# Float32 conditioning matmuls in four column groups, spread singly; small matmuls in twos; w_out in two parts

## The chip, the cores and the metric

The kernel runs on one core of one Trainium2 chip. The metric is the device time of one execution in microseconds. Nothing else runs on the chip.

## The reference: what is computed

One inference step of a one-layer decoder, for a prompt of 256 tokens and 8 sample sequences of 4 tokens, 288 tokens in all, D = 2048, everything in float32. Two recurrent mixers (HGRN2 with 16 heads, mLSTM with 8) run side by side on the input projection:

```
mod = silu(c) @ ada_w + ada_b              # c: 9 rows (prompt, 8 samples); ada_w 2048 x 12288
sh1, sc1, g1, sh2, sc2, g2 = split(mod, 6)
h = rms_norm(x) * (1 + sc1) + sh1
proj = h @ w_in                            # 2048 x 18448, split into q, f, i, g, mq, mk, mv, ...
y_a = head_norm(hgrn2(...)) * silu(hg)     # per head: state 128 x 128
y_b = head_norm(mlstm(...)) * sigmoid(mo)  # per head: state 128 x 256
merged = sigmoid(ga) * y_a + sigmoid(gb) * y_b
x = x + g1 * (merged @ w_out)              # w_out 2048 x 2048
h = rms_norm(x) * (1 + sc2) + sh2
a, g = split(h @ w_up, 2)                  # 2048 x 11264
x = x + g2 * ((gelu(conv3(a) + cb) * g) @ w_down)      # 5632 x 2048
y = rms_norm(x, final_norm_w)              # and the states after the step are outputs too
```

## The kernel before

Tokens stand along the free axis: T = 288 columns. Every weight is read once from DRAM, in chunks of 512 KB: 4 contraction tiles of 128 rows (KC) by 256 weight columns (CN), a float32 tile of 128 x 1024. SyncE issues the chunks in a fixed order into a ring `raw` of 4 slots. One block is 4 chunks: the whole contraction of 2048 for 256 output columns.

A block of kind "s" is a projection of the tokens. Its products are split in three: ScalarE makes `whi`, a copy rounded to the matmul type float32r (L781), VectorE the rest `wlo = raw - whi` (L1111), three chunks ahead of TensorE (LEAD), and TensorE does three passes per 128 x 128 weight tile, hi by hi, lo by hi, hi by lo, 24 passes of 288 columns a chunk (L449, L450, L451). A block of kind "a" is conditioning: 256 columns of ada_w, also split by both engines, in 8 passes of 256 columns a chunk (L463, with 18 stationary columns `cs`, the hi and lo parts of silu(c)). The sums land in `ps`, ScalarE copies them to `arows` (L784), `ada_turn` (L473) adds hi and lo and turns rows into columns by a product with `sel`, and VectorE adds the bias into `mod`. Slot `k % 4` of `raw` is loaded again when VectorE has made the `wlo` of the chunk four before it, for both kinds.

There are 584 s chunks and 192 a chunks. The stages, in order:

- ada1: 64 a chunks (sh1 and sc1), with the transposes of x in the first half;
- hg0 to hg3: one group of four HGRN heads each, 40 s and 8 a chunks; the heads of a group are worked off in the next stage;
- ml0 to ml3: two mLSTM heads each, 32 s and 16 a chunks; ml0 works off the last four HGRN heads, ml1 to ml3 two mLSTM heads each;
- ada2: 32 a chunks, with the last two mLSTM heads;
- out: w_out, 32 s chunks; up: 22 loops of 8 s chunks; down: 88 s chunks; then the final norm and the output.

A head is cut into steps (10 for HGRN, 12 for mLSTM), which TensorE, ScalarE, VectorE and GpSimd take at the same chunk numbers (`steps_at` spaces them evenly). TensorE's steps are generators, which yield after each small matmul: `chunk` takes one between two weight tiles, 7 a chunk, and `drain` issues all that is left at the chunk's end. Small matmuls are plain float32. The PSUM tensor `R` has 4 banks for them. The order is written out by hand on every engine; semaphores join the engines.

```
if s == 1 and b and kinds[b - 1] == "a":
    ada_turn(A0 + ada_before(b - 1, kinds), (b - 1) % 2)
drain(due)
if hook is not None:
    due = hook(k)
```

Names that come back below: `cs` stationary columns of the conditioning, `landed` DMA arrived, `lo_done` VectorE's `wlo` made, `used` TensorE done with a chunk, `bank_free` a `ps` bank read out, `Vx`/`Vxs` masked copies of a head's values for the state update, `Sst` the states of a head's 8 sub-chunks.

## Time and profile before

| | |
|---|---|
| three runs | 2757.1, 2760.88, 2763.0 us; median 2760.88 us |
| the profiled execution: its own time | 2762.37 us |
| its span | 2760.8 us |
| mean granted TensorE clock | 0.932 of full |
| TensorE busy | 2586.7 us, 94% |
| VectorE, ScalarE, GpSimd busy | 1397.2, 1285.5, 458.1 us |

TensorE is the engine that the others feed. The window rows below give for each stage its length, the busy time of TensorE, the granted clock and the share of DMA; a pass is one weight tile moved against 288 (or 256) columns, and a plain float32 matmul shows as two passes. The columns of a window row are: from and to, length, busy time (and instructions) of TensorE's matmuls, its weight loads, VectorE, ScalarE and GpSimd, granted clock, DMA share, GB/s. A timeline row has the start, the duration, engine, line, operation and tiles, output rows, the moved tile, and in brackets the idle time before it and what ended that. In a timeline row, the start of a pass less the start of the one before it is what that one costs on the path.

### The profile page before, as it was taken

To read this page: it belongs to the slowest core of one execution; us is meant where nothing else is said; L and a number is where in the kernel's file an instruction comes from. 1 tells how busy PE (TensorE), PEld (TensorE's weight loads), DVE (VectorE), ACT (ScalarE), POOL (GpSimd) and SP (SyncE) were. 2 spreads that over 40 slices of the span, in tenths; PEclk is the share of its full clock that TensorE was granted. 3 is DMA by queue.
4 is the path that set the end of the run, shared out by engine and by line. 5 is a ranking of instruction groups with operands and counts; after the bars stand their busy time and mean duration, and the time that the engine had idled before them with its cause. 6 is when DMAs were issued, how large, how long until landed. Compare 5 with 4: busy or idle time off the path is not lost.

```text
span 2760.8 us, 46789 instructions
## 1 busy us (share of the span) xinstructions
PE 2586.7 (94%) x17745; PEld 2383.9 (86%) x17745; DVE 1397.2 (51%) x1602; ACT 1285.5 (47%) x1577; POOL 458.1 (17%) x514
## 2 busy tenths in 40 slices
PE   5779999999999999999999989898999999999997
PEld 3559988888888988888888876798999999999997
DVE  4554454354344455555565456555555555544443
...
GB/s 228 269 127 203 175 161 132 140 154 138 132 154 140 146 167 164 177 178 170 153 185 192 171 170 204 178 161 158 166 167 160 167 159 172 163 199 162 168 168 89
DMA packets 424717, 460.08 MB, mean 167 GB/s; under 512 B 16676, under 2 KB 414412, under 8 KB 423330
## 3 DMA queue, kind: packets, MB, share of 16 engines
...
q14 instruction: 30, 0.25, 0.0%
...
## 4 chain that ended last, share of the span: by engine, by line
PE 79%; issue 7%; DVE 4%; DMA 4%; ACT 3%; POOL 2%; ACTq 1%; POOLq 0%; DVEq 0%; SPq 0%
PE ps L449 22%; PE ps L450 21%; PE ps L451 21%; DMA raw<-in_ada_w 2%; PE ps L463 2%; DVE wlo L1111 2%; PE R L429 1%; ACT whi L781 1%; PE R L592 1%; PE R L576 1%; PE R L653 1%; PE R L598 1%; PE R L600 1%; PE R L586 1%; PE ps L473 1%
## 5 line engine op out<-in xcount | busy, mean ns | idle before, releaser
L1111 DVE TENSOR_TENSOR wlo<-raw,whi 128x1024 fp32r<-128x1024 f32 x776 | 1036.0, 1352 | 863.4 <-ACT whi L781 848.4
L449 PE MATMUL ps<-xh,whi 128*128 128x288 f32 x3968 | 1238.7, 312 | 47.7 <-issue 29.7
L450 PE MATMUL ps<-xl,whi 128*128 128x288 f32 x3968 | 1192.4, 301 | 0.0
L451 PE MATMUL ps<-xh,wlo 128*128 128x288 f32 x3968 | 1192.1, 300 | 0.0
L781 ACT ACTIVATE whi<-raw 128x1024 fp32r<-128x1024 f32 x776 | 808.5, 1055 | 781.4 <-PE ps L451 649.2
L449 PEld LDWEIGHTS ps<-xh,whi 128*128 128x128 f32 x3968 | 769.6, 194 | 81.5 <-issue 58.7
L450 PEld LDWEIGHTS ps<-xl,whi 128*128 128x128 f32 x3968 | 767.3, 193 | 16.7 <-issue 15.1
L451 PEld LDWEIGHTS ps<-xh,wlo 128*128 128x128 f32 x3968 | 767.2, 193 | 0.0
L463 PE MATMUL ps<-whi,cs 128*18 128x256 f32 x768 | 216.6, 313 | 10.2 <-DVE wlo L1111 10.1
L463 PE MATMUL ps<-wlo,cs 128*18 128x256 f32 x768 | 212.4, 308 | 0.0
L450 PE MATMUL ps<-ffl,whi 128*128 128x288 f32 x704 | 208.4, 296 | 0.0
L451 PE MATMUL ps<-ffh,wlo 128*128 128x288 f32 x704 | 207.6, 295 | 0.0
L449 PE MATMUL ps<-ffh,whi 128*128 128x288 f32 x704 | 207.3, 295 | 0.0
L449 PEld LDWEIGHTS ps<-ffh,whi 128*128 128x128 f32 x704 | 132.5, 188 | 0.2
L450 PEld LDWEIGHTS ps<-ffl,whi 128*128 128x128 f32 x704 | 132.4, 188 | 0.0
L451 PEld LDWEIGHTS ps<-ffh,wlo 128*128 128x128 f32 x704 | 132.2, 188 | 0.0
L463 PEld LDWEIGHTS ps<-whi,cs 128*18 128x18 f32 x768 | 82.7, 108 | 54.5 <-issue 21.5
L463 PEld LDWEIGHTS ps<-wlo,cs 128*18 128x18 f32 x768 | 82.8, 108 | 22.1 <-issue 1.6
L1603 POOL COPY tails<-abuf 128x4 f32 x22 | 4.1, 187 | 421.0 <-ACT abuf L1068 421.0
L1252 DVE TENSOR_TENSOR S<-S,R 128x1024 f32<-128x1024 f32 x16 | 19.5, 1222 | 107.3 <-PE R L600 107.3
L903 ACT ACTIVATE S<-ps 128x576 f32<-128x576 f32 x40 | 26.0, 650 | 97.3 <-PE ps L451 97.3
L473 PEld LDWEIGHTS ps<-sel,arows 18*128 18x128 f32 x192 | 30.2, 222 | 40.1 <-ACT arows L784 32.1
...
## 6 DMA issues: line engine op xcount, KB each, us to landing
raw<-in_w_in SPq DMA_DIRECT2D x288, 512.0 KB, 4.0
raw<-in_ada_w SPq DMA_DIRECT2D x192, 512.0 KB, 4.7
raw<-in_w_up SPq DMA_DIRECT2D x176, 512.0 KB, 3.7
raw<-in_w_down SPq DMA_DIRECT2D x88, 512.0 KB, 3.7
raw<-in_w_out SPq DMA_DIRECT2D x32, 512.0 KB, 3.8
S<-in_state_hgrn POOLq DMA_DIRECT2D x16, 512.0 KB, 5.5
out<-S POOLq DMA_DIRECT2D x16, 512.0 KB, 4.3
...
```

The lines of the kernel that those rows point to most:

```text
L429: return nc.tensor.transpose(out, in_, ident[0:in_.shape[0], 0:in_.shape[0]])
L449: mm(o, whi[:, s, kk, cols], hi[:, kt0 + kk, :], start=first and kk == 0, stop=False)
L450: mm(o, whi[:, s, kk, cols], lo[:, kt0 + kk, :], start=False, stop=False)
L451: x = mm(o, wlo[:, s, kk, cols], hi[:, kt0 + kk, :], start=False, stop=last and kk == KC - 1)
L463: x = mm(ps[0:2 * NB, bank, 0, 0:CN], cs[:, kt0 + kk, :], w[:, s, kk, :], start=first and kk == 0 and w is whi, stop=last and kk == KC - 1 ...
L473: x = mm(ps[:, bank, 1, NB * m:NB * (m + 1)], arows[:, bank, P * m:P * (m + 1)], sel[:, :], start=True, stop=True)
L576: mm(R[:, bank, :], Kt[:, t, :], Vx[:, t].rearrange("p a b -> p (a b)"), start=True, stop=True).then_inc(hg["u"], 1)
L586: mm(R[:, 2, SUB * c:SUB * (c + 1)], Sst[:, c - 1, :], qs[:, SUB * c:SUB * (c + 1)], start=False, stop=False, skip_group_check=True)
L592: x = mm(R[:, 2, TP + LS * b:TP + LS * (b + 1)], S0[:, b, :], qt[:, TP + LS * b:TP + LS * (b + 1)], start=False, stop=b == NS - 1, skip_gr ...
L598: mm(R[:, 0, :], Kts[:, :], Vxs[:, 0:4, :].rearrange("p a b -> p (a b)"), start=True, stop=True)
L781: A(whi[:, s], raw[:, s], ACT.Copy).then_inc(hi_done, 1)
L1111: TT(wlo[:, s], raw[:, s], whi[:, s].bitcast(F32), ALU.subtract).then_inc(lo_done, 1)
```

## The change

- **Conditioning chunks.** An a chunk is no longer split. TensorE does 4 plain float32 matmuls of 256 columns (8 passes), with the contraction tile kk of the chunk into its own 32 output rows, `acc[32*kk:32*kk+32]`; `cs` is 32 wide, float32, 9 columns and zeros. It waits for the DMA alone (`landed`), and the slot of such a chunk is loaded again once TensorE has used it. ScalarE and VectorE do nothing for it. Outside ada1 the sums have a PSUM bank of their own, `ab`, so the mixers' `R` has 3 banks. `ada_turn` has contraction 128 instead of 18, and `sel` adds the four groups of rows.
- **Where they stand.** They come singly, after three s chunks or two, instead of in blocks of four: 12 in each HG stage (8 before), 12 in each ML stage (16 before), 32 in the first eight (double) loops of up (none before). Stage ada2 is gone. ada1 keeps its 64.
- **Small matmuls.** TensorE takes two small steps after every two weight tiles, 8 a chunk, and one after an a chunk. A step that isn't finished goes on in later chunks (`turns`); nothing is drained at a chunk's end. The chunk at which each step of a head is due on TensorE and on the other engines comes from tables: a head starts every 12 chunks in the HG stages, every 10 in ml0, 22 in ml1 to ml3, 11 in w_out.
- **w_out.** It comes in two parts: P1, 24 chunks, contraction tiles 0 to 11 for all eight column blocks, with the last two mLSTM heads worked off beside it; and P2, 8 chunks, tiles 12 to 15. VectorE scales P1's sums into `mixo`, and adds P2's in `second_part`, block by block; GpSimd adds `xT2`, the spilled x.
- Small: `dno` is 4 tiles instead of 16, some of the mixers' reads and order of banks differ, and an mLSTM head's first broadcast is cut in two.

The diff, cut to its core (the tables, SyncE's ring, TensorE's chunks and streams, and VectorE's w_out):

```diff
-HG_BLOCKS = "ssassssassss"
-ML_BLOCKS = "ssassassasas"
...
+HG_KINDS = "sssa" * 12 + "ssss"
+ML_KINDS = "sssa" + "sssassa" * 5 + "ssa" + "ss"
+UP_KINDS = "sssasssasssasssassss"
+THEN = "sss"
...
+HG_DUE = {0: 0, 1: 1, 2: 2, 3: 4, 5: 6, 6: 10, 7: 10, 8: 11, 9: 12}
+HG_DUE_PE = {2: 2, 4: 5, 6: 7, 8: 11}
+ML_DUE = {0: 0, 2: 3, 3: 5, 4: 6, 5: 8, 7: 14, 8: 16, 9: 18, 10: 19, 11: 20}
+ML_DUE_PE = {1: 1, 3: 4, 4: 6, 6: 9, 8: 16, 10: 19}
+OUT_DUE = {0: 0, 2: 2, 3: 3, 4: 4, 5: 5, 7: 9, 8: 10, 9: 11, 10: 11, 11: 12}
+OUT_DUE_PE = {1: 1, 3: 3, 4: 4, 6: 6, 8: 10, 10: 11}
+HG_TURNS = (2, 14, 26, 38)
+HG_TURNS_ML = (1, 11, 21, 31)
+ML_TURNS = (0, 22)
+OUT_TURNS = (0, 11)
...
-            def block256(N, b, view, col, chunks=4, first=False):
-
-                for s in range(chunks):
-                    k = chunks * b + s
+            def slot_free(N, k, kinds, tail):
+
+
+                if k >= RING:
+                    old, split = kinds[k - RING], before(kinds, k - RING + 1, "s")
+                else:
+                    old, split = tail[k], -tail[k + 1:].count("s")
+                if old == "s":
+                    sp.wait_ge(lo_done, N[2] + split)
+                else:
+                    sp.wait_ge(used, N[0] + k - RING + 1 + FREE)
...
+            def stage(N, kinds, tail, view, cols, a0=None, length=4, kt0=0):
+
+
+                for k, kind in enumerate(kinds):
+                    slot_free(N, k, kinds, tail)
+                    if kind == "s":
+                        q = before(kinds, k, "s")
+                        load(k, view, kt0 + KC * (q % length), cols[q // length])
+                    else:
+                        e = before(kinds, k, "a")
+                        load(k, ada_v, KC * (e % 4), CN * (a0 + e // 4))
...
-            def chunk(c, k, first, last, bank, hi, lo, kt0, steps=None):
-
-
-
-                pe.wait_ge(lo_done, c + 1)
+            def chunk(c, k, first, last, bank, hi, lo, kt0, steps, half=None):
+
+
+                pe.wait_ge(lo_done, c)
                 s = k % RING
                 for kk in range(KC):
+                    if half is not None and kk % 2 == 0:
+                        pe.wait_ge(xlo, half + kk // 2)
                     for m in range(2):
...
                         x = mm(o, wlo[:, s, kk, cols], hi[:, kt0 + kk, :], start=False, stop=last and kk == KC - 1)
                         if kk == KC - 1 and m == 1:
                             x.then_inc(used, 1)
-                        elif steps is not None:
-                            next(steps, None)
-
-            def ada_chunk(c, k, first, last, bank, kt0, steps):
-
-                pe.wait_ge(lo_done, c + 1)
+                    next(steps, None)
+                    next(steps, None)
+
+            def ada_chunk(c, k, first, last, acc, kt0):
+
+
                 s = k % RING
+                pe.wait_ge(landed[s], 4 * c + 16 * (k // RING + 1))
                 for kk in range(KC):
-                    for w in (whi, wlo):
-                        x = mm(ps[0:2 * NB, bank, 0, 0:CN], cs[:, kt0 + kk, :], w[:, s, kk, :], start=first and kk == 0 and w is whi,
-                               stop=last and kk == KC - 1 and w is wlo)
+                    x = mm(acc[32 * kk:32 * kk + 32, 0:CN], cs[:, kt0 + kk, :], raw[:, s, kk, :], start=first, stop=last)
                 x.then_inc(used, 1)
-                next(steps, None)
-                next(steps, None)
-
-            def ada_turn(n, bank):
+
+            def ada_turn(n, half, acc):
 
                 pe.wait_ge(ada_rows, n + 1)
                 for m in range(2):
-                    x = mm(ps[:, bank, 1, NB * m:NB * (m + 1)], arows[:, bank, P * m:P * (m + 1)], sel[:, :], start=True, stop=True)
+                    x = mm(acc[:, CN + NB * m:CN + NB * (m + 1)], arows[half][:, P * m:P * (m + 1)], sel[:, :], start=True, stop=True)
                 x.then_inc(ada_cols, 1)
...
-            def stream(N, kinds, A0, hook=None, xparts=None):
-
-
-                due = nothing()
-                for b, kind in enumerate(kinds):
-                    pe.wait_ge(bank_free[b % 2], N[1] + b // 2 + FREE)
-                    for s in range(4):
-                        k = 4 * b + s
+            now = [0]
+
+            def turns(order, step, head, i):
+
+
+                for k, j, o in order:
+                    while now[0] < k:
+                        yield
+                    yield from step(j, o, head + j, i)
+
+            def stream(N, kinds, a0=None, steps=None, length=4, kt0=0, xparts=None, halves=None):
+
+                steps = nothing() if steps is None else steps
+                for k, kind in enumerate(kinds):
+                    now[0] = k
+                    if kind == "s":
+                        q = before(kinds, k, "s")
+                        b, s = q // length, q % length
+                        if s == 0:
+                            pe.wait_ge(bank_free[b % 2], N[1] + b // 2 + FREE)
                         if xparts is not None and b == 0:
                             pe.wait_ge(xlo, xparts + s + 1)
-                        if kind == "s":
-                            chunk(N[0] + k, k, s == 0, s == 3, b % 2, xh, xl, KC * s, due)
-                        else:
-                            ada_chunk(N[0] + k, k, s == 0, s == 3, b % 2, KC * s, due)
-                        if s == 1 and b and kinds[b - 1] == "a":
-                            ada_turn(A0 + ada_before(b - 1, kinds), (b - 1) % 2)
-                        drain(due)
-                        if hook is not None:
-                            due = hook(k)
-                drain(due)
-                if kinds[-1] == "a":
-                    ada_turn(A0 + ada_before(len(kinds) - 1, kinds), (len(kinds) - 1) % 2)
+                        chunk(N[2] + q + 1, k, s == 0, s == length - 1, b % 2, xh, xl, kt0 + KC * s, steps, halves if q == 0 else None)
+                    else:
+                        e = before(kinds, k, "a")
+                        if e % 4 == 0:
+                            pe.wait_ge(ada_free, a0 - A_HG + e // 4 + FREE)
+                        ada_chunk(N[0], k, e % 4 == 0, e % 4 == 3, ab, KC * (e % 4))
+                        next(steps, None)
+                    if k >= 2 and kinds[k - 2] == "a" and before(kinds, k - 1, "a") % 4 == 0:
+                        ada_turn(a0 + before(kinds, k - 1, "a") // 4 - 1, 0, ab)
+                drain(steps)
+
...
+                stream(hg_base(i + 1), HG_KINDS, A_HG + 3 + 3 * i, turns(in_order(HG_TURNS, HG_DUE_PE), hg_step, 4 * i, i))
+            stream(ml_base(0), ML_KINDS, A_ML, turns(in_order(HG_TURNS_ML, HG_DUE_PE), hg_step, 12, 3))
...
-            def hook(k):
-                for j, o in ML_AT_ADA[k]:
-                    yield from ml_step(j, o, 6 + j, 3)
-            stream(ada2_base(0), "a" * 8, A_ADA2, hook)
-            pe.wait_ge(ml["c"], 4 * MH + FREE)
-            pe.wait_ge(ml["c2"], MH + FREE)
+                stream(ml_base(i + 1), ML_KINDS, A_ML + 3 + 3 * i, turns(in_order(ML_TURNS, ML_DUE_PE), ml_step, 2 * i, i))
+
+            stream(N_P1, "s" * 24, steps=turns(in_order(OUT_TURNS, OUT_DUE_PE), ml_step, 6, 3), length=3, xparts=4)
+            pe.wait_ge(ml["c2"], 4 * MH + FREE)
             nc.tensor.transpose(R[0:NB * MH, 1, 0:P], nnew[:].rearrange("p a b -> p (a b)"), ident[:, :]).then_inc(n_t, 1)
-
-            stream(out_base(0), "ss", 0, xparts=4)
-            with pe.Fori(1, 4) as i:
-                stream(out_base(i), "ss", 0)
+            stream(N_P2, "s" * 8, length=1, kt0=12, halves=8)
...
-            def stream(N, kinds, dst, hook):
-
-                for b, kind in enumerate(kinds):
-                    for s in range(4):
-                        k = 4 * b + s
+            def stream(N, kinds, dst=None, hook=None, each=None):
+
+                for k, kind in enumerate(kinds):
+                    if (kinds + THEN)[k + LEAD] == "s":
                         hi(N, k + LEAD)
...
+            def first_part(k, n):
+                if n % 3 == 2:
+                    u = n // 3
+                    if u == 0:
+                        dve.wait_ge(ml["sig"], 4 * 4)
+                        dve.wait_ge(ml["pre"], 2 * 4)
+                        dve.wait_ge(ada_free, 8 + FREE)
+                    b, kt = u % 2, slice(2 * u, 2 * u + 2)
+                    dve.wait_ge(used, N_P1[0] + k + 1 + FREE)
+                    TT(mixo[:, kt, 0:TP], ps[:, b, :, 0:TP], gate(u)[:, :, 0:1].to_broadcast([P, 2, TP]), ALU.mult).then_inc(x1_m, 1)
+                    TT(seq3(mixo[:, kt, TP:T], LS), seq3(ps[:, b, :, TP:T], LS), rep3(gate(u)[:, :, 1:NB], LS), ALU.mult).then_inc(bank_free[b], 1)
...
+            def second_part(k, u):
+                b, kt = u % 2, slice(2 * u, 2 * u + 2)
+                dve.wait_ge(used, N_P2[0] + k + 1 + FREE)
+                dve.wait_ge(x1_m, u + 1)
+                dve.wait_ge(bank_free[b], N_P1[1] + u // 2 + 1 + FREE)
+                for m in range(2):
+                    STT(mixo[:, 2 * u + m, 0:TP], ps[:, b, m, 0:TP], gate(u)[:, m, 0:1], mixo[:, 2 * u + m, 0:TP], ALU.mult, ALU.add).then_inc(x1_p, 1)
+                TT(seq3(x1s[:, b], LS), seq3(ps[:, b, :, TP:T], LS), rep3(gate(u)[:, :, 1:NB], LS), ALU.mult).then_inc(bank_free[b], 1)
+                dve.wait_ge(bank_free[b], N_P2[1] + u // 2 + 1 + FREE)
+                TT(mixo[:, kt, TP:T], mixo[:, kt, TP:T], x1s[:, b], ALU.add).then_inc(x1_p, 1)
+            stream(N_P2, "s" * 8, each=second_part)
```

Two places of TensorE's order. The first is in an HG stage, at the end of step 6 of a head and the first a chunk behind it. `R` holds the small results, `ps` and `ab` the streams' sums; in brackets are the semaphores waited for. Before:

```order
L583 MATMUL R<-PT,Vt 128x128
L586 MATMUL R<-qs,Sst 128x32 x7
L589 MATMUL R<-PTs,Vts 128x32
L592 MATMUL R<-qt,S 128x4 x8
L597 REGISTER_ALU
L598 MATMUL R<-Vxs,Kts 128x512 [waits hg_vx]
L600 MATMUL R<-Vxs,Kts 128x512
L459 REGISTER_ALU
L463 MATMUL ps<-whi,cs 18x256 [waits lo_done]
L463 MATMUL ps<-wlo,cs 18x256
```

The same place in the changed kernel (`xh`, `xl` are the split tokens):

```order
L654 MATMUL R<-qt,S 128x4 x2
L501 REGISTER_ALU
L503 MATMUL ab<-raw,cs 32x256 [waits landed3]
L503 MATMUL ab<-raw,cs 32x256 x3
L654 MATMUL R<-qt,S 128x4
L481 REGISTER_ALU
L489 MATMUL ps<-xh,whi 128x288 [waits lo_done]
L490 MATMUL ps<-xl,whi 128x288
L491 MATMUL ps<-xh,wlo 128x288
```

Before, the small matmuls ran out in one sequence and an a chunk followed, which waits for VectorE's `lo_done`; now two small ones precede the a chunk, which waits for the DMA, one follows it, and weight tiles of the projection come between the rest.

The second place is the first step of an mLSTM head whose work stood in ada2. Before:

```order
L463 MATMUL ps<-wlo,cs 18x256
L613 MATMUL R<-mLR,ones 128x512 [waits ml_c,ml_c2,ml_lr]
L615 MATMUL R<-mLR,ones 128x104
L617 MATMUL R<-mW 128x256 [waits ml_sig]
L619 MATMUL R<-mW 128x128
L621 MATMUL R<-mW 32x32
L429 MATMUL R<-ident,mW 128x128 x2
L429 MATMUL R<-ident,mW 32x128
L463 MATMUL ps<-whi,cs 18x256 [waits lo_done]
```

In the changed kernel it stands in P1 of w_out:

```order
L675 MATMUL R<-mLR,ones 128x328 [waits ml_c2,ml_lr]
L678 MATMUL R<-mW 128x256 [waits ml_sig]
L489 MATMUL ps<-xh,whi 128x288
L490 MATMUL ps<-xl,whi 128x288
L491 MATMUL ps<-xh,wlo 128x288
```

What moved: the head's first matmuls stood between passes of conditioning chunks, drained in one go; now two stand between weight tiles of w_out. An order row is one instruction: a plain float32 matmul is one row there and two passes in the trace.

## Rows read from the trace of the kernel before

**Rows 1.** The page: busy time, share of the span and instructions per engine.

```profile
PE 2586.7 (94%) x17745; PEld 2383.9 (86%) x17745; DVE 1397.2 (51%) x1602; ACT 1285.5 (47%) x1577; POOL 458.1 (17%) x514
```

**Rows 2.** The span in nine windows, one per stage (PEclk: mean granted clock).

```profile
28.80:189.00 160.20, 117.90 (x766) 86.19 (x767) 100.20 (x105) 99.61 (x130) 19.40 (x18) 0.82 0.74 235
189.00:332.80 143.80, 139.53 (x1040) 136.38 (x1038) 63.46 (x66) 62.14 (x75) 2.00 (x5) 0.99 0.61 174
332.80:953.90 621.10, 589.87 (x3793) 529.28 (x3794) 281.13 (x354) 289.98 (x377) 171.77 (x175) 0.90 0.48 142
953.90:1135.90 182.00, 174.78 (x1146) 152.99 (x1145) 93.97 (x121) 95.79 (x126) 57.09 (x58) 0.92 0.55 164
1135.90:1645.90 510.00, 494.05 (x3296) 443.57 (x3295) 279.44 (x271) 225.69 (x294) 103.93 (x54) 0.95 0.57 176
1645.90:1761.80 115.90, 97.77 (x477) 69.12 (x476) 70.76 (x80) 58.84 (x83) 31.88 (x20) 0.72 0.60 190
1761.80:1887.00 125.20, 110.69 (x785) 108.97 (x785) 66.97 (x71) 48.77 (x52) 10.20 (x6) 0.94 0.53 178
1887.00:2449.80 562.80, 562.80 (x4224) 562.80 (x4225) 306.39 (x398) 290.65 (x318) 31.43 (x111) 1.00 0.53 163
2449.80:2760.80 311.00, 296.62 (x2210) 292.18 (x2208) 132.84 (x135) 107.22 (x115) 23.55 (x32) 0.97 0.49 156
```

**Rows 3.** TensorE in order of time: passes of conditioning chunks, stage ada1.

```profile
34.61 0.28 PE L463 MATMUL ps<-whi,cs 128*18 128x256 f32 x1
...
35.43 0.28 PE L463 MATMUL ps<-wlo,cs 128*18 128x256 f32 x1
```

**Rows 4.** TensorE in order of time: a float32 matmul of 288 columns.

```profile
384.75 0.65 PE L603 MATMUL R<-lf,ones 128*128 128x288 f32 x2
...
385.37 0.29 PE L450 MATMUL ps<-xl,whi 128*128 128x288 f32 x1
```

**Rows 5.** TensorE in order of time: a float32 matmul with 32 output rows.

```profile
400.36 0.29 PE L451 MATMUL ps<-xh,wlo 128*128 128x288 f32 x1
400.58 0.25 PE L562 MATMUL R<-qt,kt_ 128*32 128x32 f32 x2
```

**Rows 6.** TensorE in order of time: a float32 matmul of contraction 32.

```profile
1200.05 1.12 PE L674 MATMUL R<-mVx,mK 32*128 32x512 f32 x2
...
1201.34 0.29 PE L450 MATMUL ps<-xl,whi 128*128 128x288 f32 x1
```

**Rows 7.** TensorE in order of time: small matmuls before the clock fell.

```profile
367.69 0.71 PE L583 MATMUL R<-PT,Vt 128*128 128x128 f32 x4 [1.91 <-DVE Sst L1248]
...
371.04 3.58 PE L592 MATMUL R<-qt,S 128*128 128x4 f32 x16
...
378.45 0.42 PE L463 MATMUL ps<-wlo,cs 128*18 128x256 f32 x1
```

**Rows 8.** The clock in two windows around that place.

```profile
366.00:378.20 12.20, 10.52 (x40) 7.88 (x40) 3.68 (x7) 1.35 (x2) 1.91 (x1) 0.62 0.42 129
382.90:398.00 15.10, 15.10 (x113) 14.81 (x112) 5.92 (x8) 9.74 (x13) 2.25 (x3) 1.00 0.65 202
```

**Rows 9.** TensorE in order of time: idle times, loop end and ada2.

```profile
540.89 0.40 PE L449 MATMUL ps<-xh,whi 128*128 128x288 f32 x1 [6.67 <-issue]
...
1658.58 2.07 PE L613 MATMUL R<-mLR,ones 8*128 8x512 f32 x2 [6.25 <-DVE mLR L1261]
```

**Rows 10.** Groups by line: split passes, and two producers of a head.

```profile
L1111 DVE TENSOR_TENSOR wlo<-raw,whi 128x1024 fp32r<-128x1024 f32 x776 | 1036.0, 1352 | 863.4 <-ACT whi L781 848.4 <-DMA xT<-xT_spill 9.5 <-DMA out<-Sst 2.6
L781 ACT ACTIVATE whi<-raw 128x1024 fp32r<-128x1024 f32 x776 | 808.5, 1055 | 781.4 <-PE ps L451 649.2 <-DMA raw<-in_w_in 51.1 <-DMA raw<-in_ada_w 42.1
...
L1504 POOL COPY Vx<-Vt 32x256 f32<-32x256 f32 x64 | 45.3, 707 | 48.1 <-ACT Kts L944 45.3
...
L1248 DVE SCALAR_TENSOR_TENSOR Sst<-Sst,dec,R 128x128 f32<-128x128 f32 x112 | 39.0, 348 | 4.0
```

**Rows 11.** DMA issues: KB each and us to landing, ada_w chunks.

```profile
raw<-in_ada_w SPq DMA_DIRECT2D x192, 512.0 KB, 4.7
```

More of the change, by code:

```diff
@@ L103, in down_base @@
 def down_base(i):
-    return ahead(N_DOWN, i, 44, 2)
+    return ahead(N_DOWN, i, 44, 2, 44)
 A_HG = 16
-A_ML = A_HG + 4 * HG_BLOCKS.count("a")
-A_ADA2 = A_ML + 4 * ML_BLOCKS.count("a")
-def ada_before(b, kinds):
-    return kinds[:b].count("a")
-HG_NSTEP = 10
-ML_NSTEP = 12
-def steps_at(k, first, chunks, nsteps, heads):
-    return [(j, o) for j in range(heads) for o in range(nsteps)
-            if first + (j * nsteps + o) * (chunks - first) // (heads * nsteps) == k]
+A_ML = A_HG + 4 * 3
+A_UP = A_ML + 4 * 3
@@ new lines, in down_stage @@
+            def down_stage(i):
+                stage(down_base(i), "s" * 44, "ssss", down_v, [1024 * i + CN * u for u in range(4)], length=11)
+            ada1_stage(0, first=True)
+            with sp.Fori(1, 8) as i:
+                ada1_stage(i)
+            hg_stage(0, "aaaa")
+            with sp.Fori(1, 4) as i:
+                hg_stage(i, HG_KINDS[-4:])
+            ml_stage(0, HG_KINDS[-4:])
+            with sp.Fori(1, 4) as i:
+                ml_stage(i, ML_KINDS[-4:])
+            stage(N_P1, "s" * 24, ML_KINDS[-4:], out_v, [CN * u for u in range(8)], length=3)
@@ L405, in _ @@
+            stage(N_P2, "s" * 8, "ssss", out_v, [CN * u for u in range(8)], length=1, kt0=12)
+            with sp.Fori(0, 8) as i:
+                stage(up2_base(i), UP_KINDS, "ssss", up_v, [FF * u + CN * (2 * i + p) for p in range(2) for u in range(2)], A_UP + i)
+            with sp.Fori(0, 6) as i:
+                stage(up1_base(i), "s" * 8, "ssss", up_v, [FF * u + CN * (16 + i) for u in range(2)])
             with sp.Fori(0, 2) as i:
-                for u in range(4):
-                    block256(down_base(i), u, down_v, 1024 * i + CN * u, chunks=11)
+                down_stage(i)
@@ L858, in ada1 @@
                     A(merged[:, bass.ds(4 * i, 4), :], xT[:, bass.ds(4 * i, 4), :], ACT.Square).then_inc(sq_done, 1)
-            for k in range(LEAD):
-                hi(N_ADA1, k, first=True)
-            ada1(0, True, first=True)
-            with act.Fori(1, 4) as i:
+            with act.Fori(0, 4) as i:
                 ada1(i, True)
@@ L876, in _ @@
                 ada1(i, False)
+            for k in range(LEAD):
+                hi(N_HG, k)
             modulate(1, merged, 0, KT)
@@ L1059, in _, with up_stream, each @@
             act.wait_ge(spill_1, 16)
-            with act.Fori(0, 22) as i:
-                for k in range(8):
-                    hi(up_base(i), k + LEAD)
-                    if k == 3:
-                        act.wait_ge(used, up_base(i)[0] + 4 + FREE)
+            def up_stream(N, kinds, first):
+                def each(k, n):
+                    i = first + n // 8
+                    if n % 8 == 3:
+                        act.wait_ge(used, N[0] + k + 1 + FREE)
                         act.wait_ge(ff_conv, 6 * i + FREE)
@@ L1354, in _, with up_stream, each @@
             cw = [par[:, 2, 0:44], par[:, 2, 44:88], par[:, 3, 0:44]]
-            with dve.Fori(0, 22) as i:
-                for k in range(8):
-                    lo(up_base(i), k + LEAD)
-                    if k == 4:
+            def up_stream(N, kinds, a0, first):
+                def each(k, n):
+                    i = first + n // 8
+                    if n % 8 == 4:
                         dve.wait_ge(bank_free[0], N_UP[1] + i + 1 + FREE)
```

647 lines of the change are left out of this document (331 added, 316 removed).

## The prediction

> **What bounds the kernel now.** I read the page first: TensorE is busy 94% of the span, VectorE 51%, ScalarE 47% [rows 1]. Then the nine windows by stage [rows 2]. The reader is to see three things in them. In up, TensorE runs without an idle moment at the full clock, and 562.8 us for 4224 passes is 0.133 us a pass: a chunk of 24 passes costs 3.20 us, and nothing but fewer passes helps. In ada1 it is busy 118 of 160 us: the weights' transfers and their splits set the pace. Between lie the stages with heads, where the clock stands at 0.90 to 0.95, in ada2 at 0.72, and some idle time remains. Two sums tell what is lost there. Length times (1 - clock) is at most 62 us in hg1 to hg3, 15 in ml0, 25 in ml1 to ml3, 32 in ada2. Length less busy time is 31, 7, 16 and 18 us. Where the clock falls is seen in the timeline: after a head's small matmuls, 16 passes of 4 columns in 3.58 us among them, the next conditioning pass is at half speed (0.42 us for 0.28), in a window with a granted clock of 0.62, the level of 1.2 GHz for most of it; beside projection passes it is 1.00 (2.4 GHz) [rows 3, 7, 8]. So what counts is TensorE's time: its passes, its clock, and what it waits for.
>
> **An a chunk.** Before, 8 passes. From one pass to another seven later are 0.82 us, 0.117 each, so 0.93 us a chunk [rows 3]. In the change there are 8 passes too, but of plain float32. Their price: from the start of a 288-column float32 matmul to the second projection pass behind it are 0.62 us; less one pass of 0.133, that is 0.484 for two passes, 0.24 each, two clock cycles a column [rows 4]. For 256 columns that is 0.2135 us, and 8 in sequence would be 1.71. No row shows matmuls with different groups of output rows behind each other. Upper bound: all in sequence, and going over to 32 output rows and back at the dearest switch in the trace. That is the one to contraction 32: 1.29 us from its start to the second pass behind it, less 0.133, and 0.09 before it as below, against 2 x 0.427 by columns, so 0.39 [rows 6]; sum 2.10. Lower bound: the four groups all beside each other, two passes and 0.11: 0.54. The switch I take at 0.11 in and out, since the trace has one to 32 output rows: the matmul starts 0.22 after the pass before it instead of 0.133, so 0.09 for the way in [rows 5]; the way back had hardly a cost there. For overlap I take the middle, an assumption of mine: a matmul's second pass goes to the same rows as its first and waits for it, but the next matmul's first pass is free to run beside it. That is 5 slots for 8 passes, 5 x 0.2135 + 0.11 = **1.18 us**.
>
> The Trainium skill, "TensorEngine Tiling (Array Packing)", Key Properties, says that a change of tiling mode drains the array; that speaks against 128 a chunks put singly between 128-wide passes, and the trace agrees that a switch costs, 0.09 and 0.39 us [rows 5, 6]. By the dearer one for each, the sum would be 36 us worse. Every 0.1 us of an a chunk is 12.8 us for the 128 outside ada1.
>
> **Stage by stage.**
> - ada1: the splits go. Before, a slot was free again after 4.7 us of transfer [rows 11], 1.06 of `whi` and 1.35 of `wlo` [rows 10]: 7.1 us for four slots, 1.78 a chunk. 235 GB/s at a share of 0.74 are 318 at most, 1.65 us a chunk [rows 2]. 64 x 0.13 = 8 is the least gain, the stage's whole DMA idle time, 0.26 x 160 = 42, the most; x's transposes, the norm and the gates stay. I take -15.
> - hg0: 8 a chunks at 0.93 become 12 at 1.18: +7. Its clock is 0.99 [rows 2], nothing to gain.
> - hg1 to hg3: 24 become 36: 42.5 - 22.3 = +20. Twos in place of ones, and no drain at a chunk's end, make switches more: three for each stage of them at 0.39, +4. Back comes the clock: small matmuls stand between six projection passes, not in bursts; of 62 us I take 45, since the tiny passes remain. The waits: of 31 idle us, 6.7 at each of three loop ends stay (the engine issues nothing there) [rows 9]; a head's wait for `Sst` (1.91) [rows 7] goes behind projection chunks; -9. Sum -30.
> - ml0: 16 become 12, -1; four turns at contraction 18 lose the switch of 0.39, -2; clock -11 of 15; waits -3 of 7: -17.
> - ml1 to ml3: 48 become 36, 42.5 - 44.6 = -2; twelve turns -5; clock -18 of 25; waits -5 of 16 (a chunks no longer wait for `wlo`): -30.
> - ada2 and out: 32 x 0.93 = 30 moved out, its eight turns too (-6), its idle time of 18, which begins with 6.25 us on `mLR` [rows 9], and 25 of 32 us of clock; the two heads' passes now lie in P1. Added: 3 us to split the merged tiles before P1, 5 at P1 to P2 (the last head's output to the last split, TensorE has nothing else), 1 for VectorE's three operations a block in P2 where a chunk's 3.2 us must cover them, 2 for switches. -79 + 11 = -68.
> - up: 32 x 1.18 + 8 turns at 0.43 (two float32 matmuls) = +41. Nothing hides it: TensorE has no gap there [rows 2].
> - down: nothing; its `dno` has a wait more, two blocks (70 us) behind.
>
> Sum: -15 + 7 - 30 - 17 - 30 - 68 + 41 = -112. The profiled execution took 2762.4 us, its span 2760.8, the median is 2760.9; so 2650 by either.
>
> **New waits.** An a chunk's slot comes free with TensorE, not three chunks ahead of it. An s chunk loaded there lands 4.7 us later and is needed split (2.4 more) about 7.6 us after it, two projection chunks and an a chunk on: it is just in time, in ML stages too. Queued behind a late one on ScalarE and VectorE are the heads' steps. A head's step 4 on TensorE stands 5 chunks from its start and waits for four `Vx` at 0.71 us; step 6, seven from it, for eight of `Sst` at 0.35 [rows 10]; between stand 16 and 6.4 us of projection, more than these.
>
> **Rivals.**
> - The a passes run in sequence, switches cheap: 1.82 a chunk, 128 x 0.64 = +82, and ada1's gain halved, +8: 2740. For it: no row shows two float32 passes beside each other. Against: they use different output rows.
> - Slower: in sequence with the dear switch, 2.10 a chunk, 128 x 0.92 = +118 and all of ada1's gain: **2780**. The place is TensorE in each single a chunk; it decides from about 2.05 a chunk. For it: 0.39 is what the trace has for a switch that also narrows the array [rows 6]. Against: 0.09 for 32 output rows [rows 5].
> - Full overlap: 0.56 a chunk, -79: 2570. The four matmuls would start together. The Trainium skill, "TensorE: Matmul & The Clock Gate", Part 3, has packed matmuls start some 4 ns apart; no run here shows it.
> - The tables don't fit: steps come before their operands, and TensorE, with everything in order behind it, waits at each. From 4.6 us a head over 24 heads the gain is gone; at 5, 2770. For it: PSUM has a bank less, and a row of steps on other engines stands before each wait. Against: the 16 us above.
> - The clock stays low: half of the 99 us of it don't come, and a few waits: 2705. For it: there are as many tiny passes as before.
>
> **How the numbers follow.** Chances: forecast 0.50 (its own range 2600 to 2705, from 0.8 to 1.6 a chunk), in sequence 0.15, slower 0.12, full overlap 0.06, tables 0.09, clock 0.08. The predicted time is the likeliest's, 2650. The range, 2580 to 2775, leaves out full overlap and the slower case, 18 in 100. About 0.2%, 5.5 us, is what a measurement of this kernel can tell. Faster holds the forecast, sequence, full overlap and clock cases but for 0.02 of the second: 0.77; slower the 0.12 and half of the tables' 0.09: 0.17; the rest 0.06.
>
> **What would show it.** In the changed profile: from the pass before an a chunk to the pass behind it, 1.2 us right, 1.8 or 2.1 for the rivals; up's window 604 us long, at clock 1.00; PEclk of hg1 to hg3 at 0.97 or more; no idle time before `whi` or L489 beyond 1 us outside the loop ends; ada1 at 145; ada2 and out together 173. What makes it wrong: an a chunk off by 0.5 us, or waits of 5 us and more per head behind Sst, Vx or the state updates.

## The result, and the profile after

The changed kernel takes 2779.1 us (median of 20 runs, 2759.5 to 2805.7), the kernel before 2762.0 beside it (2743.4 to 2780.2): a ratio of 1.0053, 95% interval 1.0028 to 1.0078. It is half a per cent slower; I had forecast 2650.

The page of the changed kernel, busy time per engine, which answers to [rows 1]:

```profile
PE 2519.8 (91%) x17745; PEld 2257.8 (81%) x17745; DVE 1144.0 (41%) x1435; ACT 1055.7 (38%) x1351; POOL 426.1 (15%) x524
```

TensorE is busy 67 us less than before, ScalarE 230 and VectorE 253 us less, and the span is 22 us longer: 2782.9. The engines have less to do and TensorE waits more. The windows of its stages, ada1, hg0, hg1 to hg3, ml0, ml1 to ml3, w_out (P1 and P2), up, down, with the columns of [rows 2]:

```profile
24.90:166.20 141.30, 100.84 (x768) 45.49 (x768) 22.01 (x45) 39.68 (x72) 13.97 (x18) 0.66 0.82 266
166.20:311.50 145.30, 140.20 (x1077) 132.89 (x1075) 54.30 (x59) 54.74 (x68) 2.04 (x5) 0.99 0.61 186
311.50:932.70 621.20, 572.51 (x3900) 506.69 (x3901) 254.26 (x333) 268.88 (x356) 141.04 (x175) 0.95 0.49 153
932.70:1127.80 195.10, 167.40 (x1110) 143.46 (x1108) 68.18 (x102) 73.13 (x104) 52.81 (x57) 0.92 0.45 142
1127.80:1677.60 549.80, 486.07 (x3188) 417.79 (x3188) 206.24 (x223) 182.79 (x247) 95.94 (x56) 0.92 0.48 152
1677.60:1880.90 203.30, 162.89 (x971) 144.98 (x971) 98.47 (x134) 69.68 (x92) 57.32 (x34) 0.87 0.40 131
1880.90:2471.60 590.70, 590.66 (x4513) 572.06 (x4514) 307.29 (x406) 255.89 (x298) 32.15 (x111) 1.00 0.58 184
2471.60:2782.90 311.30, 296.60 (x2210) 291.97 (x2208) 132.82 (x135) 107.45 (x115) 23.57 (x32) 0.98 0.49 156
```

Against [rows 2] and against the forecast, in us (the last column is the kernel of the third experiment, below):

| stage | before | forecast | after | both edits |
|---|---|---|---|---|
| ada1 | 160.2 | -15 | -18.9 | -17.3 |
| hg0 | 143.8 | +7 | +1.5 | -0.5 |
| hg1 to hg3 | 621.1 | -30 | +0.1 | -35.6 |
| ml0 | 182.0 | -17 | +13.1 | +3.7 |
| ml1 to ml3 | 510.0 | -30 | +39.8 | -40.3 |
| ada2 and out | 241.1 | -68 | -37.8 | -60.8 |
| up | 562.8 | +41 | +27.9 | +28.4 |
| down | 311.0 | 0 | +0.3 | +1.0 |
| before ada1 | 28.8 | 0 | -3.9 | -2.8 |
| sum | | -112 | +22.1 | -124.2 |

So the forecast comes near where there are no heads (ada1, hg0, up, down: at most 13 us off) and fails where there are. In hg1 to hg3 TensorE is busy 17 us less than before and idle 49 us instead of 31, which cancels; in ml1 to ml3 it is busy 8 us less and idle 64 us instead of 16.

What a single conditioning chunk costs, in up, TensorE in order of time:

```profile
1891.90 0.29 PE L491 MATMUL ps<-xh,wlo 128*128 128x288 f32 x1
1892.12 0.64 PE L503 MATMUL ab<-raw,cs 128*32 128x256 f32 x8
1892.69 0.40 PE L489 MATMUL ps<-xh,whi 128*128 128x288 f32 x1
1892.93 0.30 PE L490 MATMUL ps<-xl,whi 128*128 128x288 f32 x1
```

From the projection pass before it (1891.90) to the second behind it (1892.93) are 1.03 us; two passes of 0.133 belong to the projection, so the chunk costs 0.76: 0.09 to go over, 0.57 for the 8 passes, 0.11 to come back. 32 x 0.76 and 8 turns at the forecast's 0.43 are 28 us, what up has grown by.

What TensorE waited for (us in total, times, longest), the rows that matter here:

```profile
PE R L625 <- DVE kt_ L1301: 33.1, 14, 3.3
PE R L729 <- ACT hsq L1054: 27.7, 8, 4.4
...
PE R L675 <- DVE mLR L1328: 18.5, 4, 6.4
PE R L640 <- POOL Vx L1601: 16.5, 13, 6.3
...
PE R L742 <- ACT dn L1059: 10.8, 5, 4.0
```

In the same view of the kernel before, the first four of these operands stand at 3.4, 7.0, 6.3 and 9.0 us, and `dn` not at all (`kt_` belongs to an HGRN head's step 2, `mLR` to an mLSTM head's first step, `hsq` and `dn` to its late ones). And ScalarE, waiting for the weights of the projection before it can make `whi`: 237 us, where [rows 10] had 51.

```profile
ACT whi L839 <- DMA raw<-in_w_in: 237.1, 74, 9.4
```

**One wait followed back.** The longest wait for `mLR` is at the second head of an ML stage. TensorE, SyncE's queue, ScalarE and VectorE in order of time:

```profile
1217.05 0.64 PE L503 MATMUL ab<-raw,cs 128*32 128x256 f32 x8
...
1221.57 0.29 PE L491 MATMUL ps<-xh,wlo 128*128 128x288 f32 x1
1228.23 1.45 PE L675 MATMUL R<-mLR,ones 8*128 8x328 f32 x2 [6.37 <-DVE mLR L1328]
```

```profile
1217.89 2.19 SPq L401 DMA_DIRECT2D raw<-in_w_in  x3
```

```profile
1225.35 1.06 ACT L839 ACTIVATE whi<-raw 128x1024 fp32r<-128x1024 f32 x1 [7.54 <-DMA raw<-in_w_in]
```

```profile
1226.44 1.22 DVE L1175 TENSOR_TENSOR wlo<-raw,whi 128x1024 fp32r<-128x1024 f32 x1 [9.79 <-ACT whi L839]
1227.58 0.52 DVE L1328 TENSOR_SCALAR mLR<-LR,ident 8x616 f32<-8x616 f32 x1
```

The reader is to see the order. TensorE ends a conditioning chunk at 1217.7. Only then is its slot of the ring free, and SyncE, whose queue stood at that slot, issues three loads at once (1217.89), two of them into slots whose chunks had been split before. They share the DMA with a head's stores (GpSimd issues one of 1 MB at 1217.30); from 1217.9 to 1225.4 the DMA share is 0.91, at 300 GB/s, and the first load is there 7.5 us after its issue. What the stores and what the other two loads have in that, no run separates. ScalarE splits it at 1225.35, VectorE at 1226.44, and only behind that, in VectorE's written order, comes the small `mLR` that TensorE has been waiting for since 1221.9. It starts at 1228.23.

**What a wait does to the clock.** The same place in windows, the wait and the stretch behind it, and one 12 us later:

```profile
1222.00:1228.20 6.20, 0.00 (x0) 0.00 (x0) 1.76 (x3) 2.11 (x2) 0.90 (x1) 0.78 1.04 330
1228.20:1240.00 11.80, 11.77 (x61) 9.76 (x62) 2.88 (x5) 2.01 (x5) 0.00 (x0) 0.68 0.30 102
1240.00:1250.00 10.00, 10.00 (x77) 8.88 (x76) 3.30 (x6) 4.24 (x8) 0.00 (x0) 1.00 0.54 169
```

Behind the wait of 6.4 us the granted clock is 0.68 for 12 us, at 1.2 GHz for more than half of it, then 1.00 again: 11.8 x 0.32 = 3.8 us are lost on top of the wait itself.

**A wait that has nothing to do with transfers.** In the HG stages TensorE waits 2.75 us for `kt_` in nine of twelve heads. ScalarE and TensorE at one of them:

```profile
366.38 1.05 ACT L839 ACTIVATE whi<-raw 128x1024 fp32r<-128x1024 f32 x1
367.44 1.28 ACT L990 ACT_TABLE_LOAD   x1
368.73 0.63 ACT L990 ACTIVATE lf<-W,onec,lbc 128x288 f32<-128x288 f32 x1
369.27 0.63 ACT L960 ACTIVATE S<-ps 128x576 f32<-128x576 f32 x1
369.80 1.05 ACT L839 ACTIVATE whi<-raw 128x1024 fp32r<-128x1024 f32 x1
370.86 1.28 ACT L994 ACT_TABLE_LOAD   x1
372.16 0.44 ACT L994 ACTIVATE e<-bm 128x288 f32<-128x288 f32 x1
```

```profile
374.09 0.48 PE L625 MATMUL R<-qt,kt_ 128*128 128x128 f32 x2 [2.75 <-DVE kt_ L1301]
```

ScalarE has no idle time here: two table loads of 1.28 us, three copies for the streams, the logarithm and the exponentials, one behind the other; `qt` and `kt_` on VectorE follow. TensorE's step 2 is due two chunks after the head's start, and the chunk between is a conditioning chunk of 0.76 us.

### The profile page after: what moved, and what is told of

It is laid out like the page before. It is cut to its first block and busy times, and to the rows that moved or that the text cites. A ratio compares the mean times of both kernels' runs of the same rounds, so it can differ in the third digit from the quotient of the medians.

```text
span 2782.9 us, 45708 instructions
## 1 busy us (share of the span) xinstructions
PE 2519.8 (91%) x17745; PEld 2257.8 (81%) x17745; DVE 1144.0 (41%) x1435; ACT 1055.7 (38%) x1351; POOL 426.1 (15%) x524
## 5 line engine op out<-in xcount | busy, mean ns | idle before, releaser
L489 PE MATMUL ps<-xh,whi 128*128 128x288 f32 x3968 | 1273.1, 321 | 37.2 <-issue 24.5
L1175 DVE TENSOR_TENSOR wlo<-raw,whi 128x1024 fp32r<-128x1024 f32 x584 | 769.6, 1321 | 1210.0 <-ACT whi L839 1208.6
L839 ACT ACTIVATE whi<-raw 128x1024 fp32r<-128x1024 f32 x584 | 615.2, 1056 | 1153.6 <-PE ps L491 783.0
L503 PE MATMUL ab<-raw,cs 128*32 128x256 f32 x1024 | 83.1, 397 | 3.8 <-DVE mod L1190 3.8
L503 PE MATMUL ps<-raw,cs 128*32 128x256 f32 x512 | 58.7, 571 | 23.1 <-DMA raw<-in_ada_w 22.7
L1605 POOL TENSOR_TENSOR S<-S,e 128x1024 f32<-128x1024 f32 x16 | 34.1, 2128 | 268.4 <-PE R L654 268.4
L1632 POOL TENSOR_TENSOR mVx<-mV,bmask 32x2048 f32<-32x2048 f32 x8 | 31.1, 3891 | 167.5 <-ACT mV L1048 167.5
L503 PEld LDWEIGHTS ps<-raw,cs 128*32 128x32 f32 x512 | 14.4, 137 | 51.8 <-DMA raw<-in_ada_w 43.9
L640 PE MATMUL R<-Vx,Kt 128*128 128x512 f32 x64 | 37.3, 679 | 16.5 <-POOL Vx L1601 16.5
```

The source lines that it names most:

```text
L489: mm(o, whi[:, s, kk, cols], hi[:, kt0 + kk, :], start=first and kk == 0, stop=False)
L503: x = mm(acc[32 * kk:32 * kk + 32, 0:CN], cs[:, kt0 + kk, :], raw[:, s, kk, :], start=first, stop=last)
L640: mm(R[:, t, :], Kt[:, t, :], Vx[:, t].rearrange("p a b -> p (a b)"), start=True, stop=True).then_inc(hg["u"], 1)
L839: A(whi[:, s], raw[:, s], ACT.Copy).then_inc(hi_done, 1)
L1175: TT(wlo[:, s], raw[:, s], whi[:, s].bitcast(F32), ALU.subtract).then_inc(lo_done, 1)
L1605: G(S0[:, :, :], S0[:, :, :], seq(e1[:, TP:T], LS)[:, :, LS - 1:LS].to_broadcast([P, NS, P]), ALU.mult).then_inc(hg["scaled"], 1)
```

## The experiments

Times are medians of 5 or 6 runs; ratios are to the kernel before, run on the same chip beside them. Experiments 1 to 4, 8 and 9 ran on one chip, 5 to 7 on another, so these are compared by their ratios too. The stage lengths are from each kernel's profile, one execution each; for the same kernel (experiments 3 and 9) hg1 to hg3 read 585.5 and 589.9 us.

**1. A ring of their own.** The conditioning chunks of the HG and ML stages go to two slots of their own (`rawa`), so SyncE's queue never stands at a slot that only TensorE frees. The order of all instructions stays. (In up they keep the common ring; to make room, two small buffers of the heads, `bm` and `rs`, share their place with `rstd` and `lnms`.) The edit does two things at once: it takes the blocking slot out of the queue, and it gives the projection all four slots of `raw`, six in all instead of four.

```diff
+        rawa = sb("rawa", [P, 2, KC, CN], stack=hg_mem)
...
-                    slot_free(N, k, kinds, tail)
+                    elif kind == "s":
...
+                            sp.wait_ge(lo_done, N[2] + before(kinds, k, "s") - RING + 1)
...
+                        if e >= 2:
+                            sp.wait_ge(used, N[0] + pos[e - 2] + 1 + FREE)
```

> The conditioning chunks of the HG and ML stages get a ring of their own (two slots), so that SyncE's queue never stands behind a slot that only TensorE frees; the order of all instructions on the engines and the tables stay. Theory 1, the slot of an unsplit chunk blocks the queue of loads and makes splits and head steps late: ScalarE's wait for w_in transfers, 237 us in the changed kernel, falls below 90; TensorE's 18.5 us before the first broadcast of an mLSTM head (mLR) go, of its 28 us before hsq and 16 us before Vx at least half; ML stages 550 -> 520 or less; time 2730 to 2755. Theory 2, the due tables ask for operands before ScalarE and VectorE can have them whatever the transfers do: no change in these waits, 2770 to 2785.

Measured: 2713.6 us, ratio 0.9791 (0.9762 to 0.9821). Its windows, hg1 to hg3, ml0, ml1 to ml3:

```profile
313.60:930.20 616.60, 569.47 (x3901) 504.65 (x3902) 259.50 (x333) 268.35 (x356) 141.19 (x175) 0.95 0.53 153
930.20:1126.10 195.90, 168.49 (x1110) 144.84 (x1108) 68.40 (x102) 72.81 (x104) 52.31 (x58) 0.91 0.46 143
1126.10:1608.80 482.70, 457.42 (x3189) 399.94 (x3188) 205.34 (x222) 182.37 (x247) 101.22 (x55) 0.98 0.55 171
```

ml1 to ml3 fall from 549.8 to 482.7 us, their idle time from 64 to 25, the clock rises from 0.92 to 0.98. ScalarE's wait for w_in falls from 237 to 5 us:

```profile
ACT whi L870 <- DMA raw<-in_w_up: 126.0, 55, 5.6
...
ACT whi L870 <- DMA raw<-in_w_in: 5.4, 5, 3.9
```

The wait on w_up stays at 126 us and costs nothing, with the conditioning chunks of up in the common ring as in the changed kernel: up has no heads, whose operands could be late, and TensorE has no idle time there. hg1 to hg3 and ml0 hardly move (616.6, 195.9), and the 30 us before `kt_` stay. Of TensorE's waits the one for `mLR` falls from 18.5 to 0.7 us, but hsq only from 27.7 to 18.5 where I had expected half or less, and `Vx` not at all (18.6 for 16.5); the time is below the 2730 to 2755 expected. So theory 1 holds for ml1 to ml3, with more gain than I had priced, and is not the whole cause. Whether a common ring of six slots would have brought the same was not tested.

**2. Later steps.** Numbers of the tables alone.

```diff
-HG_DUE_PE = {2: 2, 4: 5, 6: 7, 8: 11}
-ML_DUE_PE = {1: 1, 3: 4, 4: 6, 6: 9, 8: 16, 10: 19}
-OUT_DUE_PE = {1: 1, 3: 3, 4: 4, 6: 6, 8: 10, 10: 11}
+HG_DUE_PE = {2: 3, 4: 6, 6: 8, 8: 11}
+ML_DUE_PE = {1: 1, 3: 4, 4: 6, 6: 9, 8: 17, 10: 20}
+OUT_DUE_PE = {1: 1, 3: 3, 4: 4, 6: 6, 8: 11, 10: 12}
```

In ML_DUE, step 11 also goes from 20 to 21.

> Only numbers of the tables: TensorE's steps 2, 4 and 6 of an HGRN head one chunk later (3, 6, 8 for 2, 5, 7), steps 8 and 10 of an mLSTM head one chunk later (17, 20 for 16, 19; in w_out 11, 12 for 10, 11). Theory 2, the tables: the 33 us before kt_, most of the 28 before hsq and of the 11 before dn go, and clock with them: 2715 to 2740, hg1 to hg3 590 for 621. Theory 1, the ring: these waits stem from late transfers and mostly turn up one chunk later: 2760 to 2780.

Measured: 2675.5 us, 0.9658 (0.9629 to 0.9687), more than theory 2 had asked for. Windows hg1 to hg3, ml1 to ml3, w_out:

```profile
315.70:899.80 584.10, 560.04 (x3900) 499.31 (x3901) 256.43 (x333) 270.52 (x356) 138.56 (x175) 0.96 0.52 164
1085.70:1594.50 508.80, 468.01 (x3189) 406.00 (x3188) 205.94 (x222) 182.23 (x247) 96.27 (x55) 0.96 0.52 164
1594.50:1776.60 182.10, 156.04 (x971) 140.20 (x971) 98.98 (x134) 69.48 (x92) 58.41 (x34) 0.89 0.45 147
```

The HG stages give 37 us, ml1 to ml3 41, w_out 21. The wait for `kt_` is down to 2.6 us, hsq to 8.8, `mLR` to 7.7 and `Vx` to 6.3, though nothing was done for the transfers (ScalarE's wait for w_in is even 297 us); a new one has come, 16 times 1.4 us for `S` before the state update. So the tables are a cause of their own, and the larger one.

**3. Both edits.**

> Both edits, own ring and later steps. If the two causes are separate their gains add: 2690 to 2715. If they are one, it is no better than the better of the two alone.

Measured: 2635.0 us, 0.9510 (0.9484 to 0.9535). That is far below the 2690 to 2715 I had expected for two separate causes, since each alone had brought more than I had priced. The gains against the changed kernel are 66 and 104 us alone and 144 together (2779.1 less each; by the ratios 72, 109 and 150). Together they bring 25 us less than their sum, about what ml1 to ml3 show: 67 and 41 us alone, 80 together. In the HG stages the gain is that of the tables. Windows hg1 to hg3, ml0, ml1 to ml3, w_out:

```profile
312.20:897.70 585.50, 559.63 (x3900) 498.84 (x3901) 255.53 (x333) 269.56 (x356) 148.52 (x175) 0.96 0.55 163
897.70:1083.40 185.70, 167.62 (x1111) 144.93 (x1109) 69.86 (x102) 72.90 (x104) 50.28 (x58) 0.91 0.48 149
1083.40:1553.10 469.70, 452.80 (x3189) 395.56 (x3188) 206.31 (x222) 182.43 (x247) 99.57 (x55) 0.99 0.55 176
1553.10:1733.40 180.30, 154.38 (x971) 138.76 (x972) 100.00 (x134) 69.50 (x92) 57.42 (x34) 0.90 0.45 149
```

ml1 to ml3 run at a clock of 0.99 with 17 us idle. This is the change as the forecast had pictured it, and it has the last column of the table above. Twelve of the 1.4 us waits for `S` are in hg1 to hg3. One of them, and the window behind it:

```profile
360.11 1.33 PE L697 MATMUL R<-lnms,ones 128*128 128x288 f32 x2 [1.40 <-DVE S L1350]
```

```profile
360.10:366.00 5.90, 5.89 (x22) 5.61 (x23) 2.17 (x3) 3.86 (x5) 1.42 (x2) 0.50 0.31 89
```

The granted clock is 1.00 until this wait begins, behind a head's small matmuls, the last of them of contraction 32, and falls to 0.50 within it. A wait of 1.4 us was followed by 6 us at 1.2 GHz, 3 us on top (at the next head by some 3 us at 1.2 GHz); so it isn't only the long waits that cost clock.

**4. One group of output rows.** The four matmuls of a conditioning chunk add into the same 32 rows; the turn takes 32 rows.

```diff
-                    x = mm(acc[32 * kk:32 * kk + 32, 0:CN], cs[:, kt0 + kk, :], raw[:, s, kk, :], start=first, stop=last)
+                    x = mm(acc[0:32, 0:CN], cs[:, kt0 + kk, :], raw[:, s, kk, :], start=first and kk == 0, stop=last and kk == KC - 1)
```

> The four matmuls of a conditioning chunk all add into the same 32 output rows (and the turn then has contraction 32). The theory that different groups of output rows run beside each other: a chunk goes from 0.77 us on the path to about 1.8, up from 591 to 624 us, turns 0.3 us dearer; in HG and ML some of it lies in waits; ada1, which waits for transfers, gains less than a third of 64 us; 2860 to 2920. If the passes were as quick for another reason (rows narrower than 128, say), up stays at 591 and the time at 2780.

Measured: 2912.5 us, 1.0509 (1.0478 to 1.0539). TensorE at one of these chunks, in up:

```profile
1993.14 0.29 PE L491 MATMUL ps<-xh,wlo 128*128 128x288 f32 x1
1993.36 1.91 PE L503 MATMUL ab<-raw,cs 128*32 128x256 f32 x8
1995.21 0.40 PE L489 MATMUL ps<-xh,whi 128*128 128x288 f32 x1
1995.44 0.29 PE L490 MATMUL ps<-xl,whi 128*128 128x288 f32 x1
```

1.85 us for the 8 passes where four groups take 0.57, and 2.03 on the path for 0.76. The groups do run beside each other: 0.57 is two passes of 256 columns (0.43) and 0.14. The Trainium skill, "TensorE: Matmul & The Clock Gate", Part 3, has packed matmuls take the time of one and some 4 ns for each further one, an estimate of 0.44 us here; I had made that the rival of full overlap. The trace has 0.57, nearer to that than to my 1.07 (5 slots).

up grows to 633.7 us (624 expected). ada1 grows by 30 us, where I had expected less than a third of 64. hg1 to hg3 have 36 of these chunks, 46 us more by the pass, and grow by 8 only, to 629.6: their idle time falls from 49 to 30 us and the granted clock rises from 0.95 to 0.99. One reason is seen at `kt_`:

```profile
420.06 0.48 PE L625 MATMUL R<-qt,kt_ 128*128 128x128 f32 x2 [1.48 <-DVE kt_ L1301]
```

Its wait is 1.48 us where it was 2.76: shorter by 1.28, what the conditioning chunk between the head's start and this step costs more. A cheap chunk had made the table tighter. The clock stood at 1.00 behind this wait of 1.48 us (420 to 426), and at 0.50 behind the one of 1.40 in experiment 3. Ahead of this one stood projection passes with a transpose now and then, ahead of that one a head's small matmuls: the length of a wait alone does not tell what it costs in clock.

**5. Ones for twos,** on the kernel with both edits.

```diff
                             x.then_inc(used, 1)
-                    next(steps, None)
-                    next(steps, None)
+                        next(steps, None)
```

> On the kernel with both edits (own ring, later steps): one small step after each weight tile instead of two after every second, still 8 a chunk. If going over between wide passes and small matmuls costs something each time, hg1 to hg3 (585 us) grow by 5 to 15 us and ml1 to ml3 (470) by as much: 2650 to 2660. If only a change to contraction 32 costs, nothing changes, since those stand alone either way: 2635.

Measured: 2647.3 us, 0.9584 (0.9561 to 0.9607). hg1 to hg3 586.5, ml1 to ml3 476.6, w_out 184.2: +1, +7, +4. TensorE's busy time grows by 6 us in each of the first two. Going over costs a little each time; the twos are worth 12 us by the medians and 17 to 20 by the ratios (against experiments 9 and 3), less in the HG stages than the first theory said.

**6. Bursts,** on the kernel with both edits: no small matmul between weight tiles, all that is due at the end of its chunk.

```diff
-                    next(steps, None)
-                    next(steps, None)
...
-                        yield
+                        yield "wait"
...
-                        next(steps, None)
+                    while next(steps, "wait") != "wait":
+                        pass
```

> On the kernel with both edits: the small matmuls of a step run out in one sequence at the end of the chunk at which they are due, none between weight tiles. The clock term of the forecast: hg1 to hg3 fall back to a granted clock of 0.90 and lose 45 us or more, ml1 to ml3 15 to 25: 2700 to 2730. If the clock in the first kernel fell for its idle times and not for the small matmuls, hg1 to hg3 stay within 15 us of 585 and the time within 2635 to 2660.

Measured: 2690.6 us, 0.9734 (0.9707 to 0.9762). Windows hg1 to hg3 and ml1 to ml3:

```profile
314.40:920.10 605.70, 583.33 (x3900) 513.04 (x3901) 247.94 (x333) 268.93 (x356) 155.81 (x175) 0.91 0.51 156
1105.50:1589.10 483.60, 472.38 (x3186) 418.25 (x3186) 190.72 (x223) 181.15 (x246) 96.18 (x56) 0.93 0.54 172
```

The granted clock falls from 0.96 to 0.91 and from 0.99 to 0.93, TensorE's busy time grows by 24 and 20 us, the stages by 20 and 14, with idle time no longer than before. The whole kernel is 56 us slower by the medians (58 to 62 by the ratios); the profiled execution, 2681.3, is one of the quick ones. The mechanism was right. By (1 - clock) x length it is worth 31 and 29 us; the stages grow by less, which would fit fewer changes between wide and small passes, and in the HG stages it is half of the 45 that I had put.

**7. The tables tuned further,** on the kernel with both edits: HG step 8 at 12, with VectorE's `Sst` step 5 at 7, and a table for ml0 with steps 4 and 6 at 7 and 9.

```diff
-HG_DUE = {0: 0, 1: 1, 2: 2, 3: 4, 5: 6, 6: 10, 7: 10, 8: 11, 9: 12}
+HG_DUE = {0: 0, 1: 1, 2: 2, 3: 4, 5: 7, 6: 11, 7: 11, 8: 12, 9: 13}
+HG_DUE_ML = {0: 0, 1: 1, 2: 2, 3: 4, 5: 7, 6: 11, 7: 11, 8: 12, 9: 12}
-HG_DUE_PE = {2: 3, 4: 6, 6: 8, 8: 11}
+HG_DUE_PE = {2: 3, 4: 6, 6: 8, 8: 12}
+HG_DUE_ML_PE = {2: 3, 4: 7, 6: 9, 8: 12}
```

> On the kernel with both edits: the last step of an HGRN head one chunk later again (12, it waits 1.4 us for the state sum 12 times), and in ml0 steps 4 and 6 at 7 and 9 (they wait 9 us for Vx there). If a wait costs itself and the clock behind it: hg1 to hg3 565 to 572 for 585, ml0 172 to 178 for 186: 2605 to 2625. If the wait is only pushed on (the later step delays what follows it in the same engines): 2630 to 2640.

Measured: 2644.8 us, 0.9575 (0.9542 to 0.9608), above both expectations and no better than the kernel with both edits (0.9510, in experiment 9 0.9524): ml0 gives 12 us (173.5), but hg1 to hg3 are 605.3, 15 to 20 longer. Two waits are back:

```profile
PE R L658 <- DVE kt_ L1334: 17.2, 13, 1.9
PE R L679 <- DVE Sst L1348: 17.0, 12, 1.9
```

`Sst` is now made a chunk later while TensorE wants it at the same chunk, and ScalarE's last step of a head (8) falls into the chunk of the next head's first, ahead of its logarithm in the written order. A one-chunk shift of one engine is a new wait on another.

**8 and 9. Only the table of ml0,** and the kernel with both edits again beside it.

```diff
+HG_DUE_ML = {0: 0, 1: 1, 2: 2, 3: 4, 5: 7, 6: 11, 7: 11, 8: 12, 9: 12}
+HG_DUE_ML_PE = {2: 3, 4: 7, 6: 9, 8: 12}
```

> The kernel with both edits, and of the edit before this one only the part in ml0: its own table, steps 4 and 6 at 7 and 9, the other engines' steps behind them. ml0 173 us for 186, the HG stages 585 as with both edits: 10 to 14 us below that kernel, run again beside it. If the loss in the HG stages of the edit before came from elsewhere than their table, they stay at 605.

> The kernel with both edits again, on the same chip as the one above, for the comparison: 2635, 0.951 of before.

Measured: 2631.4 us (2627.6 to 2633.5), 0.9509 (0.9471 to 0.9546), and 2634.6 (2631.3 to 2644.8), 0.9524 (0.9485 to 0.9563). ml0 is 175.9 for 185.2, hg1 to hg3 589.5 and 589.9. hg1 to hg3 stay as with both edits, so what experiment 7 lost there came from their own table. The 9 us of ml0 are seen in the profiles, in the medians only 3 where I had expected 10 to 14; the two intervals overlap. It has the lowest median of these, some 4.9% below the kernel before, but is not told apart from both edits.

## Why the prediction was wrong

The direction was wrong and the range missed the time by 4 us; by steps:

- **"Just in time, in ML stages too" failed.** I had named the slot that only TensorE frees and let the load behind it arrive after 4.7 us, split at 7.1, for a need at 7.6. At the measured 0.76 us a conditioning chunk the need comes at 7.2, so even that load would have had nothing to spare. But SyncE's queue stands at that slot, so three loads go out together, beside a head's stores, and the first takes 7.5 us. What is late next was named too, the heads' steps on ScalarE and VectorE, but given no price. Experiment 1 puts one on it: 67 us in ml1 to ml3 (with the two slots more that it also gives).
- **"More than these" failed: the check of the tables was incomplete.** I compared steps 4 and 6 with their slowest producer, and passed over steps 2, 8 and 10. Step 2 waits 2.75 us for a chain on ScalarE, and experiment 4 shows that this wait grows by what the conditioning chunk between gets cheaper, so 0.42 of it come with 0.76 for 1.18; in an ML head hsq and dn were late. The rival "the tables don't fit" held 0.09 and said 2770; its point of decision, 4.6 us a head, is what experiment 2 gives back: 104 us over 24 heads are 4.3.
- **Waits lowered the clock.** I had booked the clock as a gain of 99 us in all and priced a wait at its length. In ml1 to ml3, (1 - clock) x length rose from 25 to 44 us; with the ring alone, the same small matmuls and less waiting, it is 10, with both edits 5. In hg1 to hg3 it fell from 62 to 31, a gain of 31 where I had booked 45, and with both edits to 23. The bursts' own share, by experiment 6, is 24 us of TensorE's busy time in hg1 to hg3 where I had 45, and 20 in ml1 to ml3 where I had 18. Why some short waits cost clock and others none stays open.
- **The conditioning chunk was mis-sized to the other side:** 0.76 us for 1.18. With up and the 96 single ones it made the kernel some 50 us faster than forecast. The passes overlap nearly fully (0.57 us, where my 5 slots were 1.07); the switch is 0.20 in and out, not 0.11, and not the 0.39 of [rows 6].
- **Right:** ada1 (-19 for -15), down, that up grows, and, once the waits are gone, hg1 to hg3, ml1 to ml3 and w_out within some 10 us each. That this came out so near in sum, 2635 for 2650, is luck in part, two errors that cancel. With 0.76 us for a conditioning chunk the same sum gives 2596; of the 39 us that it then misses, 26 are in ml0, where waits stayed (for `Vx` 8.9 us, for `S` four times 1.4, and the clock at 0.91). The HG heads there have ten chunks instead of twelve, and 12 of the 44 are the short ones, against 12 of 52 in an HG stage.

Not settled: how much of the gain of the finer table in ml0 is real in the median; whether experiment 1 gains by the queue that no longer blocks or by the two slots more; and P1 and P2 were tried only in their tables, never as one part, so what the split of w_out itself brings was not measured.
